# Expert layer on one core: last weight matrices reordered and split by column blocks, scatter in float32r, head of the kernel reordered

## The reference, cut to what matters

```python
xn = rmsnorm(x, p['norm1_w'])
proj = xn @ p['w_in']
...
h = x + (merged @ p['w_o']).astype(x.dtype)
h = h + moe(rmsnorm(h, p['norm2_w']), ...)      # top 4 of 32 experts
...
gl = jnp.minimum(xblk @ w_gate[e] + b_gate[e], SWIGLU_LIMIT)
ul = jnp.clip(xblk @ w_up[e] + b_up[e], -SWIGLU_LIMIT, SWIGLU_LIMIT)
y  = ((ul + 1.0) * (gl * jax.nn.sigmoid(SWIGLU_ALPHA * gl))) @ w_down[e] + b_down[e]
out = sum over the experts of a token of (gate * y)
...
y_prompt = rmsnorm(hp, final_norm_w)
y_sample = rmsnorm(hs, final_norm_w)
```

## Time and profile before

| | us |
|---|---|
| median of 3 runs | 1412.71 (1412.38 to 1415.09) |
| the profiled execution, its own time | 1415.11 |
| span from its first to its last instruction | 1413.2 |
| PE busy in it | 1370.1 (97%) |
| TensorE clock granted in it, mean | 0.995 |

### The profile page before, as it was taken

One profiled execution on the slowest core, in us unless ns is written; L12 is line 12 of the kernel. 1 busy time (PEld: TensorE's weight loads), 2 busy tenths in 40 slices (PEclk: granted clock), 3 DMA queues, 4 the chain that ended last, 5 costly groups with the idle time before them and its releaser, 6 DMA issues.

```text
span 1413.2 us, 16437 instructions
## 1 busy us (share of the span) xinstructions
PE 1370.1 (97%) x7269; PEld 668.2 (47%) x7269; DVE 411.1 (29%) x773; ACT 234.4 (17%) x485; POOL 0.2 (0%) x4
## 2 busy tenths in 40 slices
PE   6999999999999999999999999999999999999996
PEld 4556677655554543434434434344343443434432
DVE  3565254263112422122121321212222212222123
ACT  2344241231001111111111111111110111111112
POOL 0000000000000000000000000000000000000000
PEclk9999999999999999999999999999999999999998
DMA  9334331011814899999999999999999999999993
GB/s 343 122 119 139 119 69 60 3 61 60 296 66 193 337 428 431 420 435 430 431 430 429 432 432 432 431 432 429 430 431 428 431 432 431 430 433 429 425 427 150
DMA packets 54792, 455.18 MB, mean 322 GB/s; under 512 B 12740, under 2 KB 22121, under 8 KB 39872
## 3 DMA queue, kind: packets, MB, share of 16 engines
q1 hardware_dynamic: 54720, 454.11, 77.7%
HBM read 449.46 MB, written 4.64 MB: 321 GB/s over the span
## 4 chain that ended last, share of the span: by engine, by line
PE 83%; DMA 12%; DVE 3%; ACT 1%; issue 0%; SPq 0%; DVEq 0%; ACTq 0%
PE ps L1096 40%; DMA sb_ring<-in_w_up_dram 11%; PE ps L763 9%; PE ps L572 9%; PE ps L1072 6%; PE ps L1133 4%; PE ps L548 3%; PE ps L989 3%; PE ps L777 3%; PE ps L612 1%; DMA sb_ring<-in_w_in_dram 1%; DVE sb_xg L1989 1%; PE ps L858 1%; PE ps L868 0%; DVE sb_h L2046 0%
## 5 line engine op out<-in xcount | busy, mean ns | idle before, releaser
L1096 PE MATMUL ps<-sb_ring,sb_xg 128*64 128x512 f32 x2048 | 453.6, 595 | 14.1 <-DMA sb_ring<-in_w_up_dram 8.7
L1096 PEld LDWEIGHTS ps<-sb_ring,sb_xg 128*64 128x64 f32 x2048 | 141.4, 137 | 280.1 <-issue 256.6
L1096 PE MATMUL ps<-sb_ring,sb_hidT 128*64 128x512 f32 x1024 | 226.0, 594 | 0.0
L2022 DVE TENSOR_TENSOR sb_hg<-ps,sb_biases 128x512 f32<-128x512 f32 x32 | 22.1, 691 | 404.0 <-PE ps L548 404.0
L1096 PEld LDWEIGHTS ps<-sb_ring,sb_hidT 128*64 128x64 f32 x1024 | 72.0, 137 | 139.9 <-issue 139.1
L763 PE MATMUL ps<-sb_xn,sb_ring 128*128 128x384 f32 x384 | 132.6, 491 | 0.0
L572 PE MATMUL ps<-sb_xn,sb_ring 128*128 128x384 f32 x384 | 128.0, 492 | 2.1 <-DMA sb_ring<-in_w_in_dram 2.1
L2046 DVE TENSOR_TENSOR sb_h<-sb_h,ps 128x512 f32<-128x512 f32 x96 | 61.5, 684 | 124.7 <-PE ps L1133 114.7
L572 PEld LDWEIGHTS ps<-sb_xn,sb_ring 128*128 128x128 f32 x384 | 73.0, 192 | 52.1 <-DVE sb_xn L1622 2.3
L763 PEld LDWEIGHTS ps<-sb_xn,sb_ring 128*128 128x128 f32 x384 | 71.1, 190 | 48.8 <-issue 3.6
L1072 PEld LDWEIGHTS ps<-sb_onehot,sb_xn 128*128 128x128 f32 x720 | 81.5, 192 | 12.2 <-issue 12.2
(11 more groups left out here) (308 smaller groups left out, 954.7 us busy)
## 6 DMA issues: line engine op xcount, KB each, us to landing
sb_ring<-in_w_down_dram SPq DMA_DIRECT2D x26, 4096.0 KB, 25.8
sb_ring<-in_w_up_dram SPq DMA_DIRECT2D x26, 4096.0 KB, 28.4
sb_ring<-in_w_gate_dram SPq DMA_DIRECT2D x25, 4096.0 KB, 30.0
sb_ring<-in_w_gate_dram SPq DMA_DIRECT2D x14, 2048.0 KB, 15.7
sb_ring<-in_w_in_dram SPq DMA_DIRECT2D x12, 2048.0 KB, 9.7
sb_ring<-in_w_up_dram SPq DMA_DIRECT2D x12, 2048.0 KB, 15.4
sb_ring<-in_w_down_dram SPq DMA_DIRECT2D x12, 2048.0 KB, 22.2
sb_ring<-in_w_br_dram SPq DMA_DIRECT2D x2, 2048.0 KB, 8.6
```

Of the source, the lines that this page charges most:

```text
L1096: last = mm(o, x(k), columns(kind, w, i, j), start=(k == 0), stop=(k == KT8 - 1))
L2022: v.tensor_tensor(kc4(hg[:, :]), kc4(bank(3)), bias, ALU.add).then_inc(S["gbd"], 1)
```

## The change

Four parts.

1. **Order and blocks at the end.** The queue's last matrices become gate 31, up 31, down 30, down 31. The second half of down 31 is loaded in two column blocks of 1 MB. Down 31 is multiplied by `down_last` per half and column block c: four matmuls, the even ones into the rows 0 to 63 of PSUM and the odd ones into the rows 64 to 127, so that the two parts of one sum lie under each other. `last_scatter(c)` then contracts over all 128 rows for one column block. The hidden values of expert 31 have a tile of their own, `hid_last`.
2. **Residual by identity.** The last sums start from `h`: `residual_placed` multiplies `ident` by `h`, six float32 matmuls of 128 x 512 columns. The final norm then reads PSUM. ACT squares from there; DVE multiplies the first 512 columns by the norm weight early (`first_columns`); the root takes the mean as its bias; ACT scales half of tiles 1 and 2, and five stores replace three.
3. **Scatter in float32r.** `slotT` holds only 0 and 1. The gate value is applied by ACT when it copies y into `y_hi` (float32r), and `y_lo` (float32r) holds what the rounding left, computed by DVE (`y_low`). Each matmul of the scatter becomes two, one with `y_hi` and one with `y_lo`, all in float32r. DVE now makes the slot tables (`slots_out`: a TENSOR_REDUCE and a TENSOR_SCALAR of 384 columns each).
4. **Head.** The identity (64 KB) is loaded from ACT's queue; the first half of piece 0 (256 columns) follows the norm weights at once, then its second half, then the rest of the constants. ACT takes half of the weighting of x; DVE's order changes. Some semaphores are merged, so PE's first turn of the convolution rows now also waits for the memory tokens.

The diff, cut to its core:

```diff
-            return {"gate": 6 * n - (2 if n else 0), "up": 6 * n + 2, "down": 6 * n + (6 if n < E - 1 else 4)}[kind]
+            return {"gate": 6 * n - (2 if n else 0), "up": 6 * n + (2 if n < E - 1 else 0),
+                    "down": 6 * n + (6 if n < E - 2 else 8 if n == E - 2 else 4)}[kind]
...
-            dma(cst[:, :], A["consts"]).then_inc(S["cst"], 16)
-            trunk_piece(0)
+            for k, signal in enumerate((S["cols_in"], loaded[0])):
+                cols = slice(256 * k, 256 * k + 256)
+                dma(piece(TRUNK_SLOT[0])[:, :, cols], trunk[0][:, :, cols]).then_inc(signal, 16)
+            dma(cst[:, P:CONST_WIDTH], A["consts"][:, P:CONST_WIDTH]).then_inc(S["vec_in"], 16)
...
+            for c, signal in enumerate((piece_in[(q + 1) % 8], loaded[5])):
+                block = slice(512 * c, 512 * c + 512)
+                dma(slot(q + 1).rearrange("p (t n) -> p t n", t=4)[:, :, block], wd[E - 1, :, 4:8, block]).then_inc(signal, 16)
...
+            def placed(a, i, banks, first, final):
+                for part in (y_hi, y_lo):
+                    for j in range(2):
+                        own = slice(64 * j, 64 * j + 64)
+                        last = mm(bank(banks[j]), slotT[own, i, a * P:(a + 1) * P], part[own, i, :],
+                                  start=(first and part is y_hi), stop=(final and part is y_lo))
+                return last
...
-                    for j in range(2):
-                        last = mm(bank(banks[j]), pgT[64 * j:64 * j + 64, i, a * P:(a + 1) * P],
-                                  y_sb[64 * j:64 * j + 64, i, :], start=(i == 0 and not bias), stop=(i == items - 1))
+                    last = placed(a, i, banks, i == 0 and not bias, i == items - 1)
...
+            gate_turned(E - 2)
+            scattered(E // 2 - 1)
+            product("up", order("up", E - 2), 1, gathered(0), landed)
+            up_turned(E - 2)
+            product("gate", order("gate", E - 1), 0, gathered(1), landed)
+            both_slots_turned(E // 2 - 1)
+            gate_turned(E - 1)
+            product("up", order("up", E - 1), 1, gathered(1), landed)
+            pe.wait_ge(S["hf"], E - 1)
+            up_turned(E - 1)
...
+            for a in range(TILES):
+                for c in range(2):
+                    residual_placed(a, c)
+            pe.wait_ge(S["ylo"], E - 2)
+            product("down", order("down", E - 2), 2, hidden, landed)
...
+            down_last(0, 0)
+            pe.wait_ge(S["ylo"], E - 1)
+            down_last(0, 1).then_inc(S["used"], 1)
+            for a in range(TILES):
+                placed(a, 0, acc_banks(E // 2, a), False, False)
+            pe.wait_ge(piece_in[(q + 1) % 8], landed(q + 1))
+            down_last(1, 0).then_inc(S["used"], 1)
+            pe.wait_ge(S["ylo"], E)
+            last_scatter(0)
+            pe.wait_ge(loaded[5], 16 * (TRUNK_SLOT.count(5) + 1))
+            down_last(1, 1).then_inc(S["used"], 1)
+            pe.wait_ge(S["ylo"], E + 1)
+            last_scatter(1)
...
+            nc.scalar.dma_start(cst[:, 0:P], A["consts"][:, 0:P]).then_inc(S["cst"], 16)
```

More of the change, by code:

```diff
@@ L9 @@
 I32 = mybir.dt.int32
+F32R = mybir.dt.float32r
 ALU = mybir.AluOpType
@@ L1146, in item, with hidden_last, down_last @@
-            def item(n, last=False):
+            def hidden_last(k):
+                return hid_last[:, k % 4, k // 4, :]
+            def down_last(half_, c):
+                w = slot(order("down", E - 1) + half_).rearrange("p (t n) -> p t n", t=4)
+                for i in range(4):
+                    j = i % 2
+                    last = mm(bank(4 - 2 * c)[64 * j:64 * j + 64, :], hidden_last(4 * half_ + i), w[:, i, 512 * c:512 * c + 512],
+                              start=(half_ == 0 and i < 2), stop=(half_ == 1 and i >= 2))
+                return last
@@ new lines, in residual_placed, with last_scatter @@
+            def residual_placed(a, c, final=False):
+                return mm(bank(acc_banks(E // 2, a)[c]), ident, h[:, a, 512 * c:512 * c + 512], start=True, stop=final)
+            def last_scatter(c):
+                for a in range(TILES):
+                    for part in (y_hi, y_lo):
+                        last = mm(bank(acc_banks(E // 2, a)[c]), slotT[:, 1, a * P:(a + 1) * P], part[:, 1 - c, :],
+                                  start=False, stop=(part is y_lo))
+                    last.then_inc(S["acc"], 1)
@@ L1147, in item @@
+            def item(n):
                 m, i = divmod(n, 2)
                 gate_turned(n)
-                if n != E - 2:
-                    product("up", order("up", n), 1, gathered(i), landed)
+                product("up", order("up", n), 1, gathered(i), landed)
                 if i == 0:
                     if n:
[L1153 to L1159, removed]
-                                pe.wait_ge(S["accrd"], 6 * m - 4)
-                            scatter(m, a, acc_banks(m, a), bias=BIAS_ROUND.get(m) == a)
-                    if n == E - 2:
-                        product("up", order("up", n), 1, gathered(i), landed)
-                elif not last:
+                        scattered(m)
+                else:
@@ L1227, in _ @@
                             scatter(r, a, (6, 7), items=1)
+                pe.wait_ge(S["hadd"], 2 * TILES + 1)
+                for a in range(TILES):
+                    for c in range(2):
+                        last = residual_placed(a, c, final=True)
+                last.then_inc(S["redo"], 1)
         @block.scalar
@@ L1243, in x_root, with x_weighted @@
                 f(small[:, 46 + t:47 + t], small[:, 40 + t:41 + t], ACT.Sqrt).then_inc(S["rt5"], 1)
+            def x_weighted(t):
+                act.wait_ge(S["xtr"], t + 1)
+                for k in range(4):
+                    last = f(xnT[:, k, t * P:(t + 1) * P], bank(2 * t)[:, k * P:(k + 1) * P], ACT.Copy, scale=norms[:, k:k + 1])
+                last.then_inc(S["xTa"], 1)
             x_square(0)
@@ L1247, in _ @@
             x_root(0)
+            x_root(1)
             x_square(2)
-            x_root(1)
             x_root(2)
+            act.wait_ge(S["cst"], 32)
+            for t in range(TILES):
+                x_weighted(t)
             def xp_sample(c):
```

325 lines of the change are left out of this document (193 added, 132 removed).

## The result

| | before | after |
|---|---|---|
| median of 20 executions each, same chip | 1414.26 us (1411.49 to 1416.68) | 1416.84 us (1414.75 to 1419.46) |
| ratio, 95% interval | | 1.0018, 1.0010 to 1.0025 |
| profiled execution: span; own time | 1413.2; 1415.11 us | 1414.5; 1416.39 us |
| mean granted clock | 0.995 | 0.995 |

The kernel became 0.18% slower, about 2.6 us in the medians. I had forecast no change, -0.7 us.

What follows compares the result with a forecast made beforehand. Weight transfers bound the expert stage; PE's work from up 29 on and the end set the finish. Head -1.8, PE's list +6.0, end -4.95 gave -0.7: 1412.0 us from 1412.71, range 1408.2 to 1417.8 (own range 1410 to 1414.5).

Steps and rivals of the forecast that it cites:

- The price of float32r: Scatter calls on PE: one pass out of float32's four, 0.11 us per call in a pair, 0.22 alone.
- half-price rival: Scatter calls: float32r costs half a float32 call, 0.22 us paired, 0.44 alone; +5.2 us, 1417.2 us; chance 0.20.
- Head, -1.8: Kernel start: earlier first columns let the first product start at 14.1 us, not 15.90; -1.8 us.
- faster rival: Mainly the head: tile 2 not late and PE's clock kept, -5.1 in place of -1.8 us, 1408.7; chance 0.26.
- Scatter of round 15, -0.55: Scatter ahead of up 30: later start on y_lo but cheaper calls, up 30 at 1355.4, not 1355.95; -0.55 us.
- Residual and the scatter of expert 30, +2.45: PE ahead of down 31: six identity calls add 5.3 us, expert 30's scatter leaves there, -2.85 us.
- Down 31 in pieces, +4.1: Within down 31: expert 30's scatter 1.3, PE standing for eviction 1.5, first block's scatter 1.3; +4.1 us.
- The end, -4.95: Last product to end of span: 9.95 us in place of 14.9, with 3.42 behind the last output; -4.95 us.
- slower rival: Scatter calls: float32r at half a float32 call's price, not a quarter; +5.2 us, 1417.2 us; chance 0.20.

Runs made afterwards that it cites:

- no_residual: The changed kernel without the six identity products, so h is left out of the output; ratio 0.9976 to the kernel before.
- no_pe_branch: The changed kernel without the overflow read and branch behind PE's last product, overflow rounds left out on PE; ratio 1.0008 to the kernel before.
- three_stores: The changed kernel with three output stores of 512 KB in place of five; ratio 1.0012 to the kernel before.
- blocks_together: The changed kernel with down 31's second-block product ahead of the first block's last scatter, both blocks evicted before the first's squares; ratio 1.0003 to the kernel before.
- head_only: The kernel before with the change's new head alone; ratio 0.9976 to the kernel before.
- head_no_branch: The kernel before with the new head and without the overflow read and branch at PE's end; ratio 0.9982 to the kernel before.

## Why the prediction was wrong

It was right in where the time goes: the transfers keep the expert stage, PE's list behind up 29 and the end decide, and PE never waits for a weight behind that landing. By its own steps:

- **The price of float32r: right.** 0.115 us per paired call and 0.23 alone, where I took 0.11 and 0.22; the half-price rival is gone. The Trainium skill (FP8 and Floating Point Precision, TensorE Precision Notes) says four passes for float32, and the trace agrees: 0.881 against 0.23.
- **Head, -1.8: too small, and near by luck.** The product started later than I had it (15.19, not 14.1): tile 2 was scaled at 11.98 and not at 11.3, and its turns were done at 13.95, 1.9 us behind their start where I had 1.46 and 0.1. So the start moved by 0.7 us and not by 1.8. But the clock, which I had kept for a rival, held, which gave 1.7: together -2.4 behind the first products. The clock's half of my faster rival came true, the other half (tile 2 not late) did not.
- **Scatter of round 15, -0.55: nothing came.** `y_lo` was there 29.96 us behind the landing, where I had 30.0. But the eight calls of one tile, from the first to its result, take 1.22 and 1.20 us on the chain where I had 0.9: they start every 0.23 us a pair, but the last pair of the second group starts at 1352.15, 0.80 us behind the first, and lasts another 0.40. With the waits of 1.91 and 0.53 us ahead of them up 30 is no earlier: 33.86 us behind the landing, 33.90 before.
- **Residual and the scatter of expert 30, +2.45: right,** +2.4 measured; 5.15 for 5.3. That no_residual won all of it back shows the term.
- **Down 31 in pieces, +4.1: 0.9 too small.** Its pieces take 3.51 + 1.89 + 1.89 = 7.29, twelve calls 1.58 and not 1.3, the first block's six 1.65 and not 1.3.
- **The end, -4.95: this step failed.** It was priced as the last output value plus 3.42 us, taken from a kernel whose stores waited for their values, with gaps in the transfers. In the changed kernel all 1.57 MB are ready within 1.7 us of the first store, and the transfers have no gap, so the first store and the bytes set the end: without the fetch 6.35 us behind it (no_pe_branch), which is 1413.4, 1.2 us later than the last value plus 3.42. Another 1.1 us are the instruction fetch. 1.2 + 1.1 are the 2.3 us by which this term was off. In the kernel before the two prices gave the same end (1406.78 + 6.35 = 1413.1, and the span is 1413.2), so its rows could not tell them apart. The 1.1 us are shown by taking the branch out. The 1.2 us are read from the transfers and from three_stores; no run moved the last value alone.

The errors of the tail add up to 0.5 + 0.9 + 2.3 - 0.1 = 3.6 us, against 0.6 us more from the head than forecast; in the profile the landing is 1.6 us earlier than forecast, of which 1.0 is not the head's. Without the 2.3 us of the end the profiles would have differed by -1.0 us and not by +1.3: this term decides the sign. My slower rival had the wrong mechanism, a price per call, and the one that decided, a tail in which the stores' transfer and not the last value is the bound, was not on the list. The remark that SP issues the five stores beside ACT was true and beside the point.

By the profiles the ledger closes: the head gives 2.4 us, the tail costs 95.8 - 91.0 = 4.8, and the medians show +2.6 (interval 1.4 to 3.5).

What stays open is the size of the clock's part. In two of the profiles with the changed tail (three_stores and no_pe_branch), round 15's scatter behind its 1.90 us wait ran partly at half clock and took 0.8 and 0.9 us more; in the other three that have this wait (after, no_residual, blocks_together) it did not. And in every kernel here the executions with a lower mean clock tend to be longer: of the 20 of the changed kernel, the nine at 0.995 or 0.996 have a median of 1415.0 us and the six at 0.990 to 0.992 one of 1418.7; of the kernel before, on the chip of head_only, it is 1413.6 for 0.995 to 0.997 and 1420.9 for 0.989 to 0.992. Where the clock fell in the executions without a profile is not on record, so differences of 1 us between two medians can come from how often it fell.

## What to carry to other kernels

Price the end of a kernel by two bounds, last value plus its own small transfer and first store plus the whole transfer, and take the later; a term copied from a tail that is bound by its values is no price for one that is bound by its bytes. A shortcut that needs a second half (`y_lo`) is only worth its cycles where some product covers that half; look for the places where the cover is missing before counting it. And when work is moved from a side engine onto the bound engine, as the residual's additions here, its full price there (5.15 us) has to be set against what the chain at the end really gives back (2.6 us).

## What the hardware did that I had not expected

- The branch at the end of PE's program brings a fetch of instructions (16 KB, q8; gone in no_pe_branch), which made the stores end 1.1 us later where it came among them (7.47 against 6.35 us), and cost nothing that shows where it came earlier (6.5 us with and without it, head_only and head_no_branch).
- Waits of the same length had different ends for the clock. Ahead of round 15's scatter PE stood 1.90 or 1.91 us in seven profiles: in five of them the pairs of calls start every 0.23 us behind it (1.00), in two (three_stores, no_pe_branch) the clock went to half. Ahead of an up product a wait of 1.85 us left it at 7.09 us three times in the changed kernel's profile (at 789, 848 and 1142 us), and one of 1.86 us in blocks_together made it 8.78. Two rows of no_pe_branch (columns of rows 1), round 15's scatter, where a pair of calls starts every 0.42 us in place of 0.23:

```profile
1349.00:1351.00 2.00, 0.35 (x3) 0.16 (x2) 1.58 (x3) 0.84 (x2) 0.00 (x0) 1.00 0.98 418
1351.00:1353.00 2.00, 1.75 (x8) 1.47 (x10) 0.89 (x2) 0.20 (x1) 0.00 (x0) 0.57 1.00 426
```

- One such drop in the steady rounds cost nothing: behind the 2.78 us wait at 907 us an up product took 8.78 in place of 7.09 us, but from there to the next wait for up weights no product waited for a transfer, and that wait, at 994.83, lies on the chain that ended last. So PE had caught up:

```profile
907.35 8.78 PE ps L1120 x32
...
965.35 29.44 DMA sb_ring<-in_w_up_dram
994.83 7.09 PE ps L1120 x32
```
